# 32 of 256 tokens served by indexed row transfers in a two-layer encoder with product-key experts

## The reference

```
q = (xt @ wq).reshape(T, 8, 2, 128)
s = einsum('thpc,phnc->thpn', q, subkeys)        # two scores per head against 128 keys each
top_s, top_i = top_k(s, 16)                      # 16 x 16 candidates per head, the best 16 taken
expert = ...                                     # first key * 128 + second key: one of 16384 experts
g = softmax(best_s)
hid = gelu(einsum('td,thkd->thk', xb, u[eb]))    # eb: the 8 x 16 experts of each token
out = einsum('thk,thkd->td', g * hid, v[eb])
```

## Time and profile before

| | us |
|---|---|
| median of three runs | 2163.23 (2159.97 to 2164.56) |
| span of the profiled execution, first to last instruction | 2156.3 |
| the profiled execution's own time | not given apart; the median lies 6.9 over the span |
| TensorE busy | 2138.4 |
| VectorE busy | 1546.2 |
| ScalarE busy | 1207.9 |
| GpSimd busy | 703.6 |

### The profile page before, as it was taken

One profiled execution on the slowest core, in us unless ns is written; L12 is line 12 of the kernel. 1 busy time (PEld: TensorE's weight loads), 2 busy tenths in 40 slices (PEclk: granted clock), 3 DMA queues, 4 the chain that ended last, 5 costly groups with the idle time before them and its releaser, 6 DMA issues.

```text
span 2156.3 us, 39034 instructions
## 1 busy us (share of the span) xinstructions
PE 2138.4 (99%) x13024; PEld 1891.9 (88%) x13024; DVE 1546.2 (72%) x2748; ACT 1207.9 (56%) x1988; POOL 703.6 (33%) x342
## 2 busy tenths in 40 slices
PE   8999999999999999999999999999999999999999
PEld 7777889999999988888877778899999999888887
DVE  5867869977777666666568678699767786666665
ACT  5855455477877533333367554555778785333332
POOL 1300016877777500000023000178777774000000
PEclk9999999999999999999999999999999999999999
DMA  6444554554444555555654445545545445555654
GB/s 239 155 142 144 195 172 151 181 181 157 164 161 161 177 192 191 191 193 194 195 199 156 140 148 194 166 156 183 172 163 165 163 160 180 191 193 191 191 194 155
DMA packets 103756, 377.13 MB, mean 175 GB/s; under 512 B 11760, under 2 KB 11760, under 8 KB 103152
## 3 DMA queue, kind: packets, MB, share of 16 engines
q1 hardware_dynamic: 102528, 371.24, 52.6%
q10 hardware_dynamic: 1136, 4.79, 0.6%
HBM read 374.94 MB, written 1.05 MB: 174 GB/s over the span
## 4 chain that ended last, share of the span: by engine, by line
PE 94%; DVE 3%; ACT 2%; issue 1%; DMA 0%; POOL 0%; ACTq 0%; SPq 0%; POOLq 0%; DVEq 0%
PE ps L517 28%; PE ps L519 28%; PE ps L518 28%; PE ps L869 3%; PE ps L525 3%; PE ps L527 1%; PE ps L536 1%; DVE w_lo L1299 1%; PE ps L652 1%; PE ps L830 1%; ACT w_hi L969 1%; PE ps L732 0%; PE ps L611 0%; DVE arena L1401 0%; DVE keep_lo L1422 0%
## 5 line engine op out<-in xcount | busy, mean ns | idle before, releaser
L1168 ACT ACTIVATE w_hi<-raw 128x1024 fp32r<-128x1024 f32 x512 | 523.5, 1054 | 438.6 <-PE ps L519 437.9
L502 POOL TENSOR_TENSOR w_lo<-raw,w_hi 128x1024 fp32r<-128x1024 f32 x264 | 634.1, 2417 | 267.9 <-ACT w_hi L1168 267.9
L517 PE MATMUL ps<-hT,w_hi 128*128 128x256 f32 x2048 | 580.1, 283 | 0.0
L518 PE MATMUL ps<-hT,w_hi 128*128 128x256 f32 x2048 | 579.6, 283 | 0.0
L519 PE MATMUL ps<-hT,w_lo 128*128 128x256 f32 x2048 | 579.6, 283 | 0.0
L517 PE MATMUL ps<-w_hi,wgt_hi 128*128 128x512 f32 x1024 | 398.5, 389 | 0.0
L518 PE MATMUL ps<-w_lo,wgt_hi 128*128 128x512 f32 x1024 | 398.4, 389 | 0.0
L519 PE MATMUL ps<-w_hi,wgt_lo 128*128 128x512 f32 x1024 | 398.4, 389 | 0.0
L518 PEld LDWEIGHTS ps<-hT,w_hi 128*128 128x128 f32 x2048 | 393.2, 192 | 0.0
L519 PEld LDWEIGHTS ps<-hT,w_lo 128*128 128x128 f32 x2048 | 393.2, 192 | 0.0
L517 PEld LDWEIGHTS ps<-hT,w_hi 128*128 128x128 f32 x2048 | 393.2, 192 | 0.0
(11 more groups left out here) (202 smaller groups left out, 2885.1 us busy)
## 6 DMA issues: line engine op xcount, KB each, us to landing
raw<-in_w_u SPq DMA_DIRECT2D x256, 512.0 KB, 3.4
raw<-in_w_v SPq DMA_DIRECT2D x256, 512.0 KB, 3.7
raw<-in_stream SPq DMA_DIRECT2D x192, 512.0 KB, 3.5
arena<-in_bias ACTq DMA_DIRECT2D x2, 1024.0 KB, 5.6
arena<-in_subk ACTq DMA_DIRECT2D x2, 1024.0 KB, 5.0
x<-in_x SPq DMA_DIRECT2D x4, 256.0 KB, 4.3
out<-x SPq DMA_DIRECT2D x4, 256.0 KB, 2.2
arena<-in_params ACTq DMA_DIRECT2D x2, 283.5 KB, 3.6
```

The lines of the kernel that those rows point to most:

```text
L502: nc.gpsimd.tensor_tensor(w_lo[:, i, :], raw[:, i, :], w_hi[:, i, :].bitcast(F), ALU.subtract).then_inc(early_ready.sem, 1)
L517: mm(out_, left[0], right[0], start=start, stop=False, skip_group_check=group)
L518: mm(out_, left[0], right[1], start=False, stop=False, skip_group_check=group)
L1168: f(w_hi[:, slot, :], raw[:, slot, :], ACT.Copy).then_inc(hi_ready.sem, 1)
```

## The change

- The first 32 tokens (`SPARSE`) leave the dense path; 224 (`DENSE`) stay. Up products stream 224 columns, and there are 56 gate groups.
- The 32 tokens' experts are fetched by rows. The tokens' 128 choices lie on the partitions as 4 parts of 32 choices (`PARTS`), so that one gather of 128 rows of 4 KB serves all 32 tokens with 4 experts each: 32 gathers of `u` rows and 32 of `v` rows, issued by GpSimd as indirect transfers into a ring of 3 buffers. VectorE takes a dot of each `u` tile with the tokens (`dot`, an operation with a summed output) and later multiplies each `v` tile with its weight and accumulates (`add_rows`). Ten dots lie behind filled pairs 11, 14, ... 38, the other 22 behind down pairs 2 to 23, and the 32 accumulations behind down pairs 26 to 57.
- Early pairs are 24, filled pairs 40.
- In the down products the expert rows' chunks are stationary and the gate weights stream: per key 8 chunks, each a matmul of 448 columns (high and low weights side by side) and one of 224. The result is transposed (width by tokens, eight banks), so at the end ScalarE copies the low sums, VectorE adds them, TensorE transposes back, and VectorE adds to x.
- ScalarE rounds the gate weights from pair 2 on (`round_weights`). `w_lo` is made by VectorE for even down pairs and by GpSimd for odd ones and the first.

The core of the diff:

```diff
-EARLY = 20
+EARLY = 24
+SPARSE = 32
+DENSE = T - SPARSE
+PARTS = P // SPARSE
+GROUPS = DENSE // 4
+RING = 4 * SPARSE // 32 - 1
+GATHERS = 2 * SPARSE
+STEPS = list(range(11, FILL - 1, 3))
+STEPS += [FILL + 2 + i for i in range(SPARSE - len(STEPS))]
+FIRST_SUM = STEPS[-1] + 3 - FILL
+STEPS += [FILL + FIRST_SUM + i for i in range(SPARSE)]
...
+                def gather(q):
+                    table, s = (u_rows, q) if q < SPARSE else (w_v.rearrange("l p k n -> (l p k) n"), q - SPARSE)
+                    if q >= RING:
+                        pool.wait_ge(g_taken.sem, g_taken.at(layer, q - RING + 1))
+                        pool.sem_inc(seen_pool, 1)
+                    nc.gpsimd.indirect_dma_start(
+                        out=ring[q % RING], out_offset=None, in_=table,
+                        in_offset=bass.IndirectOffsetOnAxis(ap=row_of[:, s:s + 1], axis=0)
+                        ).then_inc(gathered[q % RING].sem, 16)
...
+                for pair in range(PAIRS):
+                    if pair == 0 or pair % 2:
+                        for e in range(2):
+                            split_e(N_U + 2 * pair + e, 2 * (pair % 2) + e)
+                    while asked < GATHERS and STEPS[asked - RING] + 2 <= FILL + pair:
+                        gather(asked)
+                        asked += 1
...
-                                       [h[:, kc, :] for h in (hT_hi, hT_lo)], start=(kc == 0), stop=(kc == KC - 1))
+                                       [h[:, kc, SPARSE:T] for h in (hT_hi, hT_lo)],
+                                       start=(kc == 0), stop=(kc == KC - 1))
...
+                def expert_chunk(k, e, c, first=False):
+                    dims = slice(c * P, (c + 1) * P)
+                    mm(ps[:, c, 0:2 * DENSE], w_hi[:, 2 * k + e, dims], wgt[:, k, e, :, :].rearrange("p a b -> p (a b)"),
+                       start=first, stop=False, skip_group_check=True)
+                    return mm(ps[:, c, 0:DENSE], w_lo[:, 2 * k + e, dims], wgt[:, k, e, 0, :],
+                              start=False, stop=False, skip_group_check=True)
...
+                for j in range(PARTS):
+                    act.dma_start(xs[j * SPARSE:(j + 1) * SPARSE, :], x[0:SPARSE, 0, :]).then_inc(xs_loaded.sem, 16)
...
+                def round_weights(it, k, at):
+                    act.wait_ge(v_mm.sem, v_mm.at(layer, it * 2 + (k - 1)))
+                    act.sem_inc(seen_act, 1)
+                    f(wgt[:, k, :, 0, :], G[:, bass.ds(it * 4 + at, 2), :], ACT.Copy).then_inc(wgt_hi.sem, 1)
+                    for e in range(2):
+                        split_e(2 * k + e, it + (N_STREAM + N_U) // SLOTS, v_mm, it * 2 + (k - 1))
...
+                def dot(s):
+                    landed(s)
+                    rows_ = ring[s % RING]
+                    v.scalar_tensor_tensor(out=rows_, in0=rows_, scalar=1.0, in1=xs, op0=ALU.mult, op1=ALU.mult,
+                                           accum_out=hid[:, s:s + 1]).then_inc(g_taken.sem, 1)
+                def add_rows(s):
+                    q = SPARSE + s
+                    landed(q)
+                    rows_ = ring[q % RING]
+                    if s == 0:
+                        last = v.tensor_scalar(xs, rows_, hid[:, 0:1], None, ALU.mult)
+                    else:
+                        dve.wait_ge(g_taken.sem, g_taken.at(layer, q))
+                        last = v.scalar_tensor_tensor(out=xs, in0=rows_, scalar=hid[:, s:s + 1], in1=xs,
+                                                      op0=ALU.mult, op1=ALU.add)
+                    last.then_inc(g_taken.sem, 1)
...
+                for p in range(2, PAIRS):
+                    weigh(p)
+                    if p % 2 == 0:
                         for e in range(2):
+                            split_e(2 * p + e, e)
+                    if p == FIRST_SUM:
+                        share_out()
+                    if FILL + p in STEPS:
+                        q = STEPS.index(FILL + p)
+                        if q < SPARSE:
+                            dot(q)
+                        else:
+                            add_rows(q - SPARSE)
...
+                turn(0)
+                turn(1)
+                turn(2)
+                add_experts(0)
+                turn(3)
```

More of the change, by code:

```diff
@@ L103, in one, with pool_v, dve_v, build @@
         self.n += 1
-def build(nc, x_in, stream, w_u, w_v, subk, params, bias_in, out):
+def pool_v(pair, e):
+    return N_U + (0 if pair == 0 else pair + 1) + e
+def dve_v(pair, e):
+    return N_STREAM + pair - 2 + e
+def build(nc, x_in, stream, w_u, w_v, subk, params, bias_in, u_rows, gain_rows, out):
     F = mybir.dt.float32
@@ L906, in expert_out @@
                         pe.wait_ge(signal.sem, signal.at(layer, n + (e + 1)))
[L907 to L911, removed]
-                                               start=(first and e == 0), stop=False,
-                                               group=True)
+                        for c in range(KC):
+                            last = expert_chunk(k, e, c)
@@ L923, in _ @@
+                expert_out(PAIRS - 2, 0, w_ready, dve_v(PAIRS - 2, 0))
                 pe.wait_ge(wgt_ready.sem, wgt_ready.at(layer, PAIRS))
[L924 to L934 removed]
+                pe.wait_ge(early_ready.sem, early_ready.at(layer, N_POOL))
@@ L937, in _ @@
+                for n in range(1, 4):
+                    out_transposes(n)
+                    if n == 2 and layer + 1 < LAYERS:
+                        x_there(1, layer + 1)
+                        norm_transposes(lambda n: x_there(n, layer + 1), (0, 1))
         @block.scalar
@@ new lines, in _, with turn, add_experts @@
+                dve.sem_inc(seen_dve, 1)
+                own.one(v.memset(outT[:, :, 0:SPARSE], 0.0).then_inc(dve_chain, 1))
+                dve.wait_ge(dve_chain, own.n)
+                def turn(n):
+                    dve.wait_ge(v_lows.sem, v_lows.at(layer, n + 1))
+                    v.tensor_tensor(outT[:, 2 * n:2 * n + 2, SPARSE:T], ps[:, 2 * n:2 * n + 2, 0:DENSE],
+                                    v_low[:, 2 * n:2 * n + 2, :], ALU.add).then_inc(outT_ready.sem, 1)
+                def add_experts(half):
+                    dve.wait_ge(outT_mm.sem, outT_mm.at(layer, 2 * half + 2))
+                    dve.sem_inc(seen_dve, 1)
+                    for t in range(TT):
+                        tile = x_tile(2 * half + t).rearrange("p (a b) -> p a b", a=4)
+                        v.tensor_tensor(tile, tile, ps[:, 4 * half:4 * half + 4, t * P:(t + 1) * P], ALU.add
+                                        ).then_inc(x_ready[2 * half + t].sem, 16)
```

281 lines of the change are left out of this document (190 added, 91 removed).

## The result

The changed kernel takes 2210.0 us (median of 4 runs, 2203.6 to 2214.0), the kernel before 2161.8 us in the same series (4 runs, 2160.0 to 2164.6). The ratio is 1.022, with a 95% interval of 1.020 to 1.024: slower, where 2132.5 us was forecast.

The account below looks back on a forecast made before the run. TensorE was taken as the bound, with columns streamed as time. The terms -61.4, -7.7, +18.4, +10, +8 and +2 sum to -30.7 us on the median of 2163.2: 2132.5 us, range 2045 to 2198.

Parts of the forecast that it names:

- Part 3: Down products: 54 pairs at 5.7 us and 10 at 4.96, 357.4 us a layer against 348.2, +18.4 us for two layers.
- The pair of 5.7 us: Down pair with a row operation, set by VectorE and GpSimd taking turns: 5.7 us, lower end 5.35, upper end 6.1.
- The pairs without a row operation at 4.96 us: Ten down pairs a layer, taken at the time of TensorE's products alone: 4.96 us each instead of 5.44.
- Part 1: Up products of 224 columns instead of 256: 0.110 us each for 0.120, 6144 products, -61.4 us.
- Part 2: 56 gate groups instead of 64: -7.7 us; moving pairs from filled to early is free.
- Part 4: Ten dots among the filled pairs delay tiles that TensorE awaits: +5 us a layer, +10 in all.
- Part 5: Small pieces: index work hidden, DMA issues before the query products +2, end and turn of the layers with transposes +8.
- A: Rival: turns don't bind, every down pair 4.96 us, no loss among filled pairs: 2043 us, chance 0.22.
- B: Rival: each gather holds GpSimd for 3 us, down pairs 6.35 us, filled stage loses too: 2225 us, chance 0.11.
- C: Rival: the accumulating dot on VectorE takes double time, 2.2 us: 2188 us, chance 0.08.
- D: Rival: up products of 224 columns cost what 256 do: 2194 us, chance 0.07.

Follow-up runs that it names:

- dense_only: Changed kernel without the dots and accumulations (one element copied for each) and without 61 of 64 gathers a layer: 2089.5 us, ratio 0.966.
- deep_ring: Changed kernel with three more buffers for gathered rows in the down stage, gathers asked for up to four pairs ahead: 2122.7 us, ratio 0.983.
- v_splits: Changed kernel with VectorE making the down stage's low halves from the third pair on, GpSimd there only issuing gathers: 2082.1 us, ratio 0.9625.
- idle_splits: The kernel with VectorE making the down stage's low halves, plus two unused GpSimd subtractions in every odd pair: 2177.1 us, ratio 1.007.
- v_one_ahead: The kernel with VectorE making the low halves, each down-stage gather also waiting for the row operation just before its own: 2411.9 us, ratio 1.115.
- narrower: Changed kernel with up products of 192 columns in early pairs and 160 in filled pairs instead of 224: 2209.2 us in one run.

## Why the prediction was wrong

**The step that failed** is the down stage's sum in Part 3, "54 x 5.7 + 10 x 4.96", in both of its terms. By the starts of the wide products, the first layer's down stage divides like this (the second layer is within 0.3 us of it except for the changed kernel's middle, 335.8, and dense_only's end, 41.7):

| kernel | first two pairs | the 56 between, 54 with a row operation (none in dense_only) | a pair there | last six pairs |
|---|---|---|---|---|
| forecast | 9.9 | 317.7 | 5.67 | 29.8 |
| changed kernel | 11.9 | 340.2 | 6.07 | 43.2 |
| deep_ring | 11.0 | 293.4 | 5.24 | 43.4 |
| dense_only | 10.7 | 280.7 | 5.01 | 40.3 |
| v_splits | 11.9 | 280.7 | 5.01 | 35.0 |

**The pair of 5.7 us** was built from turns alone. Of the late rows the prediction says: "Each is asked for about one pair before its use, so a late one delays VectorE's next low part; that is inside the 6.1". I had seen the wait and did not price it. The runs show the opposite weights: without lateness (deep_ring) a pair takes 5.24 us, below even the lower end of 5.35, so the turns cost at most 0.23 us over the products' own 5.01 and were priced at 0.7; lateness, with the turns that it brings on, adds 0.83 us, 91 us for the two stages of deep_ring together. That the sum, 6.07, comes out near the upper end of 6.1 is luck. The price needed only a landing time: one pair of 5 us against a loop of 7 us means that VectorE stands still, and its stop throws its operations into GpSimd's next subtractions. The transfer's landing (5.3 to 5.7 us) appears nowhere in my sum; the page of the kernel before had 3.7 us for a load of weights, and I took only the issue's price. The 112 pairs together missed by 41 us.

**The pairs without a row operation at 4.96 us** are the second failed term. The last six took 43.2 us for 29.8, 27 us over the two layers, a third of the whole miss. The fold (11.2 us of VectorE) stops TensorE for 6.7 us, the pair behind it runs in part at a granted clock of 0.50 (it takes 7.5 us), and ahead of the last pair TensorE waits 1.8 us more for a low half of GpSimd's. The fold was in the change and in no term of the sum. It is read from the traces; no run took it away. With the 56 pairs alone wrong the time would have come out near 2173 us, inside the range; the last pairs and Part 1 took it beyond 2198.

**What stood still also slowed.** The down products of the changed kernel are busy 345.3 us where the same ones in v_splits are busy 323.4, at a granted clock of 0.94 against 0.99. The difference to v_splits, 67 us of stage, thus divides into 45 us of idle TensorE and 22 us of products at the lower clock after the waits. At a granted clock of 0.50 a wide and a narrow product take 0.59 us from start to start (four such in 2.35 us from 972.14), at 1.00 they take 0.313 (25 in 7.83 us from 948.08). The second part I left out wholly. No experiment parts it from the first, but the pairs show it too: behind seven of the twelve waits of the first layer, the next pair took 6.5 to 7.9 us for the same products as the others' 5.1, with no wait in it.

**Part 1** was 10 us too good: 0.1117 us a product (12 steps in 1.34 us) for 0.110, so 6144 x 0.0083 = 51 us instead of 61.4. The same pace makes a down pair 5.01 us by itself for 4.96, 7 us over both layers, part of the miss above. **Part 2** fits the books. **Part 4** measured 7.4 us for 10. **Part 5** was 14.4 for 10, mostly at the turn of the layers: 7.5 us pass between the last down product and the first of the next layer's, forecast as 3, and 1.5 a layer for the transposes.

```profile
1105.76 1.03 PE L627 MATMUL ps<-ident,arena 128*128 128x128 f32 x8
1107.85 1.09 PE L627 MATMUL ps<-ident,x 128*128 128x128 f32 x8 [1.05 <-DVE x L2067]
1108.78 0.60 PE L627 MATMUL ps<-ident,arena 128*128 128x128 f32 x4
1110.27 0.66 PE L627 MATMUL ps<-ident,x 128*128 128x128 f32 x4 [0.89 <-DVE x L2067]
1113.29 0.60 PE L608 MATMUL ps<-w_hi,hT 128*128 128x512 f32 x1 [2.37 <-DVE hT L1457]
```

TensorE and VectorE alternate there, with three waits of 4.3 us in all. Why the first layer's up products start 3.6 us later was not tried.

**The rivals.** Slower had been given 0.34, and the measured time lies outside the range of 2045 to 2198. A (turns don't bind, 2043 us) failed on idle_splits, though the turns bound less than I had them; v_splits came nearest to it by taking them away. B named the right queue and the wrong price: a gather holds GpSimd 1.2 to 1.3 us, not 3, and its harm is its landing, not its issue; its 2225 us were near by accident. C: the accumulating dot takes 1.21 us where GpSimd is silent (v_splits), the plain form 1.28, so it isn't the slower of the two. D failed on the pace of 0.112.

## What to carry to other kernels

Price an asynchronous step by its whole loop, from the signal that frees its buffer through every instruction ahead of its issue in that queue to its landing, and hold that against the distance at which it is asked for. A helper engine whose work holds up the one that it relieves can cost more than it takes over: here two subtractions of GpSimd (4.89 us) took 3.3 us of VectorE; VectorE alone did all the work with time to spare (263 of 328 us busy), and 128 us came back. Count the work that comes once a stage as well: a fold of 11 us on VectorE, in no term of the sum, stopped TensorE for 7 in each layer. When two waits feed each other, take each away alone and then both; if the gains don't add, the loop between them is the thing to cut, and the order of three lines in a queue may do it.

## What the runs showed of the hardware

- An indirect transfer of 128 rows of 4 KB holds GpSimd for 1.2 to 1.3 us in the mean in the changed kernel (0.93 to 1.95), and its rows land 5.3 to 5.7 us after its start (medians); with the handovers, 7.1 us from the end of the operation that it waits for to the use of its rows (8.35 less the row operation's 1.28, v_one_ahead). In deep_ring, where each is asked for up to four pairs ahead, the median landing into the down stage's buffers was 7.1 to 8.0 us.
- Products with alternating 128 x 128 weights keep a pace of 0.112 us at 160, 192 (narrower) and 224 columns (the changed kernel) alike, 0.110 at 128 and 0.120 at 256 (the kernel before). On 128 x 64 weights, 128 columns keep 0.055 (the kernel before).
- GpSimd's subtractions hold up VectorE's operations on two SBUF operands even where nothing depends on either: 4.89 us of useless subtractions took 3.3 us of VectorE and almost nothing of GpSimd (idle_splits).
- TensorE's granted clock fell to 0.50 in nine stretches of the changed kernel's first down stage: at seven of its twelve waits of 3.2 us, at the one of 6.7 us and behind one of 1.8 us; and in none of the up stage before it, where it waited 2.6 us in all.
